# Gated units: one fp32 product from the ring in place of three fp32r products on split pieces, and seven ring slots for the experts

## What is computed

```python
def swiglu(x, w1, w3, w2):
    return (jax.nn.silu(x @ w1) * (x @ w3)) @ w2
...
    for e in range(N_EXPERTS):
        out = out + combine[:, e:e + 1].astype(t.dtype) * swiglu(t, w1[e], w3[e], w2[e])
...
        u = depthwise_conv_2(h @ w_up[l], up_conv_w[l], up_conv_b[l], 1, 1)
        gate, val = jnp.split(u, 2, axis=-1)
        x = x + (jax.nn.gelu(gate) * val) @ w_down[l]
```

## Time and profile before

| | |
|---|---|
| median of 3 runs | 2473.58 us (2473.04 to 2474.61) |
| profiled execution | 2470.8 us, span 2468.7 us |
| TensorE / VectorE / ScalarE / GpSimd busy | 89% / 58% / 46% / 51% |
| weight DMA | 485.11 MB, mean 197 GB/s |
| mean granted TensorE clock | 0.946 |

### The profile page before, as it was taken

One profiled execution on the slowest core, in us unless ns is written; L12 is line 12 of the kernel. 1 busy time (PEld: TensorE's weight loads), 2 busy tenths in 40 slices (PEclk: granted clock), 3 DMA queues, 4 the chain that ended last, 5 costly groups with the idle time before them and its releaser, 6 DMA issues.

```text
span 2468.7 us, 26815 instructions
## 1 busy us (share of the span) xinstructions
PE 2201.0 (89%) x10576; PEld 1742.6 (71%) x10576; DVE 1433.9 (58%) x1744; ACT 1140.9 (46%) x1156; POOL 1248.4 (51%) x555
## 2 busy tenths in 40 slices
PE   8988699899886898989989898999989896887998
PEld 7477488775764676767767677888767674656997
DVE  1773533337735676767857676334468576454665
ACT  2152244321421574756657474443357474344554
POOL 0333255303230695959769595455478594203553
PEclk9999899989997999999999999999999998978999
DMA  7210254532002696978969697455469696203551
GB/s 290 98 35 1 77 214 169 188 112 86 30 1 86 231 365 230 367 273 325 356 241 366 231 366 262 171 195 180 171 243 362 236 360 223 102 35 154 205 178 45
DMA packets 208105, 485.11 MB, mean 197 GB/s; under 512 B 9168, under 2 KB 13008, under 8 KB 206928
## 3 DMA queue, kind: packets, MB, share of 16 engines
q1 hardware_dynamic: 207952, 483.02, 54.3%
HBM read 481.96 MB, written 1.05 MB: 196 GB/s over the span
## 4 chain that ended last, share of the span: by engine, by line
PE 78%; DVE 13%; issue 4%; ACT 3%; SPq 1%; DMA 1%; POOL 0%; DVEq 0%; ACTq 0%
PE bank L920 19%; PE bank L922 18%; PE bank L921 18%; PE bank L549 10%; PE bank L741 4%; DVE b_arena L1215 3%; PE bank L556 3%; ACT e_hi L2012 2%; DVE e_lo L1667 2%; DVE b_arena L1209 2%; PE bank L1023 1%; PE bank L702 1%; DVE b_X L1209 1%; PE bank L1102 1%; DVE b_arena L1212 1%
## 5 line engine op out<-in xcount | busy, mean ns | idle before, releaser
L2619 POOL TENSOR_TENSOR e_lo<-b_ring,e_hi 128x512 fp32r<-128x512 f32 (+3 forms) x407 | 1096.5, 2715 | 700.7 <-ACT e_hi L2012 700.6
L1667 DVE TENSOR_TENSOR e_lo<-b_ring,e_hi 128x1536 fp32r<-128x1536 f32 (+1 forms) x403 | 794.2, 1975 | 461.3 <-ACT e_hi L2012 460.5
L2012 ACT ACTIVATE e_hi<-b_ring 128x2048 fp32r<-128x2048 f32 (+1 forms) x407 | 776.3, 1911 | 408.4 <-PE bank L922 369.8
L920 PE MATMUL bank<-e_hi,e_xh 128*128 128x512 f32 (+1 forms) x1200 | 484.2, 403 | 5.7 <-DVE e_xl L1671 1.4
L922 PE MATMUL bank<-e_hi,e_xl 128*128 128x512 f32 (+1 forms) x1200 | 471.5, 393 | 0.0
L921 PE MATMUL bank<-e_lo,e_xh 128*128 128x512 f32 (+1 forms) x1200 | 471.4, 393 | 0.0
L920 PEld LDWEIGHTS bank<-e_hi,e_xh 128*128 128x128 f32 x1200 | 230.1, 192 | 74.0 <-issue 25.2
L920 PE MATMUL bank<-e_hi,e_th 128*128 128x512 f32 x688 | 271.7, 395 | 2.5 <-DVE e_tl L1671 2.4
L922 PE MATMUL bank<-e_hi,e_tl 128*128 128x512 f32 x688 | 268.8, 391 | 0.0
L921 PE MATMUL bank<-e_lo,e_th 128*128 128x512 f32 x688 | 268.2, 390 | 0.0
L922 PEld LDWEIGHTS bank<-e_hi,e_xl 128*128 128x128 f32 x1200 | 229.6, 191 | 50.0
(11 more groups left out here) (207 smaller groups left out, 2413.3 us busy)
## 6 DMA issues: line engine op xcount, KB each, us to landing
b_ring<-in_moe_w SPq DMA_DIRECT2D x168, 2048.0 KB, 8.2
b_ring<-in_w_in SPq DMA_DIRECT2D x15, 2048.0 KB, 8.2
b_ring<-in_ffn_w SPq DMA_DIRECT2D x15, 2048.0 KB, 7.9
b_ring<-in_w_up SPq DMA_DIRECT2D x12, 2048.0 KB, 8.0
b_ring<-in_w_down SPq DMA_DIRECT2D x6, 2048.0 KB, 8.8
b_ring<-in_w_o SPq DMA_DIRECT2D x4, 2048.0 KB, 7.9
b_gain<-in_gains SPq DMA_DIRECT2D x7, 1024.0 KB, 4.8
b_ring<-in_w_out SPq DMA_DIRECT2D x2, 2048.0 KB, 8.5
```

The lines of the kernel that those rows point to most:

```text
L920: e.matmul(out, ah, bh, start=first, stop=False)
L1667: e.tensor_tensor(lo[:, 0:at], raw[:, 0:at], r32(hi[:, 0:at]), ALU.subtract).then_inc(lo_dve.sem)
L2012: return e.activation(out, x, ACT.Copy)
L2619: e.tensor_tensor(lo[:, at:], raw[:, at:], r32(hi[:, at:]), ALU.subtract).then_inc(lo_pool.sem)
```

## The change

The gated products become single fp32 matmuls on the ring's own slots; `e_hi`, `e_lo`, `e_xl`, `e_tl` and all splitting on ScalarE, VectorE and GpSimd go; GpSimd has nothing left in the gated stages. The activations are plain fp32 copies (`e_x`, `e_th`, `XT`). A use is one piece instead of two, and a slot is free when TensorE has read it (`w_read`, `up_mm`, `down_mm`). The space freed in the arena holds three more slots while the experts' weights pass (7 instead of 4). SyncE's small loads are moved, and up to two more uses are issued ahead of the gain loads in front of layer 0's feed-forward and of `last_feed`.

```diff
@@ pe
-            def three(out, ah, al, bh, bl, first, last):
-                e.matmul(out, ah, bh, start=first, stop=False)
-                e.matmul(out, ah, bl, start=False, stop=False)
-                return e.matmul(out, al, bh, start=False, stop=last)
...
+                    e.wait_ge(*ring_in(at))
                     for s in range(tiles):
                         if kind == "d":
...
+                            e.wait_ge(th_out.sem, 2 * (unit + u) + (s + 1) * inc)
+                            w2 = slot(at, 1024, w // 128)
+                            for c in range(w // 128):
                                 for h in range(2):
...
+                                    ins = e.matmul(bank[4 + 2 * s + h][:, :], e_th[s][:, c, :], w2[:, c, half(h)],
+                                                   start=u == 0 and c == 0, stop=u == n - 1 and c == w // 128 - 1)
...
+                        b, wt = bank[s] if kind == "w1" else bank[2 + s], slot(at, w)
+                        ins = sums(b[:, 0:w], [(x[s][:, c, :], wt[:, c, :]) for c in range(8)])
+                    ins.then_inc(w_read.sem)
@@ last_feed
-                                ins = three(bank[b][:, 256 * f:256 * f + 256], h3[:, c, tok(f)], l3[:, c, tok(f)],
-                                            xh2[:, :, c, :], xl2[:, :, c, :], c == 0, c == 7)
+                        ins = sums(bank[b][:, 256 * f:256 * f + 256], cols_of(w, 2 * q + f))
@@ vector, scalar and gpsimd
-                    if p + 2 < ends:
-                        split_rest(p + 2, 4 if tail and p + 2 >= at + 42 else 6)
...
-                    if p + 2 < ends:
-                        split_round(p + 2)
...
-            for ex in range(NE):
-                for i in range(42):
-                    split_rest(MOE_P + 42 * ex + i, 4 if ex and i < 2 else 6)
@@ ring
+        ring = [r[:, :] for r in fixed] + [arena[:, 22240 - SLOT * i:22240 - SLOT * (i - 1)] for i in range(NM - NR, 0, -1)]
...
+        order[4:4] = range(NR, NM)
+        for i in range(NR, NM):
+            held[i] = [wo_mm(1)]
...
+        order[:] = [i for i in order if i < NR]
```

More of the change, by code:

```diff
@@ L185, in steps_of @@
     for u in range(n + 1):
[L186 to L205, removed]
+        out += [("T", u - 1)] * (u > 0) + [("w1", u), ("w3", u)] * (u < n) + [("d", u - 1)] * (u > 0)
     return out
@@ L439, in two_blocks, with gated_uses @@
         q2_mul, lru_ix = later(sq_out, 2, 2), later(g_wide, 2, 8)
-        up_mid, up_gelu, up_h = later(XT_out, 2, 2), later(u_out, 2, 1), later(mix_cv, 2, 1)
-        up_conv, up_mul, up_l = later(w_out, 2, 2), later(v_out, 2, 1), later(o_out, 2, 1)
-        uses = []
+        up_mm, down_mm = later(inv_P, 2, 2), later(inv_XP, 2, 1)
+        up_mid, up_gelu = later(XT_out, 2, 2), later(u_out, 2, 1)
+        up_conv, up_mul = later(w_out, 2, 2), later(v_out, 2, 1)
+        uses, order, held, loads = [], list(range(NR)), {}, [0] * NM
         def use(src, *read):
[L448 to L454, removed]
+            i = order.pop(0)
+            order.append(i)
+            loads[i] += 16
+            uses.append((src, i, held.get(i, ()), (s_ring[i], loads[i])))
+            held[i] = read
+        def gated_uses(w1, w3, w2, widths):
+            n = len(widths)
             for u in range(n + 1):
@@ L1186, in last_feed @@
-                    ins.then_inc(piece.sem)
+                                for h in range(2):
+                                    ins = e.matmul(bank[4 + 2 * t + h][:, :], h4[:, 2 * c + t, :], w[:, 2 * q + c, half(h)],
+                                                   start=k == 0 and c == 0, stop=k == npair - 1 and c == 1)
+                        ins.then_inc(down_mm.sem)
+                        continue
+                    b, w = up.take(), slot(n)
+                    for f in range(2):
+                        ins = sums(bank[b][:, 256 * f:256 * f + 256], cols_of(w, 2 * q + f))
@@ L2260, in mixer, with gated @@
                 weave(mixer_attention(l), mixer_delta(l), mixer_conv(l))
-            def split_round(p):
-                raw, hi, _, _ = split_views(p, 0)
-                e.wait_ge(*pieces[p][0])
-                if p >= NH:
-                    e.wait_ge(*piece(p - NH))
-                copy(hi, raw).then_inc(w_hi.sem)
-            def gated(widths, at, unit, tiles, ends, tail=None):
-                n, p, inc = len(widths), at, 2 // tiles
-                for kind, u, hf in steps_of(widths):
+            def gated(widths, at, unit, tiles, tail=None):
+                n, inc = len(widths), 2 // tiles
+                for kind, u in steps_of(widths):
                     w = widths[u]
@@ L2705, in sp @@
             load_gain(5, rms_out(0))
[L2706 removed]
+            load(FF2_AT + 4)
             load_gain(6, rms_out(1))
```

371 lines of the change are left out of this document (124 added, 247 removed).

## The result

The changed kernel takes 2746.64 us (median of 4 runs, 2744.19 to 2751.56), the kernel before beside it 2473.31 (4 runs, 2469.98 to 2474.61): a ratio of 1.111, 95% interval 1.109 to 1.1129. That is slower by 273 us. The forecast was 2775, so the rise was put 28 us too high.

A forecast was written before the change was run, and what follows sets the result against it. TensorE was taken as the bound, with transfers nearly level in one-tile experts. Dearer products +361 us less 60 us of waits gave +301 on the 2473.6 us median: 2775 us, range 2738 to 2822.

The forecast's parts named there:

- Price of a product: Gated stages: one fp32 matmul takes 0.859 us against 0.681 for three fp32r, +0.178 per full product, +0.074 per 256-wide one.
- rival 2: Gated products: each costs four full fp32r passes, 0.908 us, giving 2885 us; chance 0.04.
- Count and sum by stage: Gated stages: 1856 full products add 330 us (layer 0 44, experts 269, last feed-forward 17), 416 narrow ones 31; together +361.
- `e_h` and `e_y`: Gated stages: TensorE's waits for these VectorE results shrink about 1 us each with VectorE idle, -19 us.
- Layer norm 0 and the last feed-forward: Their starts: without splitting, slow small operations and copies go; -6.8 and -0.7 us at the first, -6.5 and -0.8 at the last.
- Late pieces: Experts with one tile: waits for late split pieces go, 0.45 us for 6 units of 7 experts, -19 us.
- Start of the experts: First expert's selection: without ScalarE's copies and VectorE's split ahead of it, 7.2 of the 9.56 us wait goes.
- Branch stops and "seven slots ... so 0": Seams between experts: stops behind branches stay at 6 to 9 us, and the seven ring slots gain 0.
- Rival 1: Seams: the stop behind a branch falls to 2 us, gaining 48 us, for 2727 us; chance 0.10.
- Start of an expert: Transposes of `e_G` to first T, one tile: 16 x 0.178 less 1.44 us of `e_h` wait, +1.4 us.
- the term put at 0: Seams between experts: no change in time was counted there, 0 us.

The follow-up runs named there:

- the reordered kernel: Kernel before, with VectorE's products, copies and picks ahead of its splits, ScalarE's last roundings behind the norm, GpSimd's split at layer norm 0 held: 2460.92 us.
- the busy GpSimd: Changed kernel with four useless 128x1024 GpSimd subtractions beside the layer norm of layer 0: 2751.03 us, one run.
- two matmuls of three: Kernel before without the product of the tokens' high part and the weights' low part, all splitting and transfers kept: 2295.46 us.
- the load held: One weight load per seam between experts held until TensorE begins the next expert: 2461.88 us on the kernel before, 2748.86 on the changed kernel.
- the early jump: TensorE's last wait of an expert moved behind the branch: 2440.46 us on the kernel before, 2734.07 on the changed kernel.

## Why the prediction was right, and where it was off

- *Price of a product:* right. 0.860 us against 0.859, in the unit with two tiles (3.8 times the 0.227 of one fp32r matmul, so rival 2's four full ones at 0.908 did not come); the last feed-forward is 249 us as computed.
- *Count and sum by stage:* right. From the first product of layer 0's feed-forward to the next norm's transposes it is +46.3 us (245.05 against 198.77), where 44 + 2.4 were forecast. The expert with two tiles grew by 58.8, where 59.8 less a few us of waits was.
- *`e_h` and `e_y`:* -19, as forecast, and the reordered kernel shows that the cause is VectorE's queue.
- *Layer norm 0 and the last feed-forward:* 7.4 and 7.9 us (7.2 of the wait, 0.7 of the copy), near the forecast (7.5 and 7.3); the busy GpSimd and the stretched rows showed the mechanism of the first. That of the last was not tested apart.
- *Late pieces:* the step took 0.45 us of a unit where the rows leave 0.57: 17.37 - 16.8. All of it went, 0.85 us more per expert than counted with the rounding of T, some 6 in all. That splitting was its cause was not shown: moving VectorE's products ahead of its splits left the unit at 17.37, and with two matmuls of three it came to 16.56 beside a DMA at 0.97.
- *Start of the experts:* the wait fell by 7.4, where 7.2 was forecast; the stop behind the first branch fell too, from 2.94 to 0.91 us, and was not counted.
- *Branch stops and "seven slots ... so 0":* this is the step that failed, in size. The slots are worth nothing, as said. But the stops did not stay: -9.9 in TensorE's waits. The prediction took their length for that of a jump alone; part of it was time in which a weight transfer was under way, and in the changed kernel that transfer starts earlier and is nearly over at the jump. Rival 1 named a shorter stop, down to 2 us and worth 48. Its causes are not borne out (with four slots the stops are as short, and with the load held they are nearly as short over the old code); its gain came to a fifth.
- *Start of an expert:* +0.87 us where +1.4 was computed, 4 in all over seven; not followed up.

The late pieces (6), the first branch (2), the seams (9.4 by elapsed time: 7.9 of stops, 1.5 of clock) and the starts of the experts' units (4) make 21 of the 24 us by which the span's rise missed the sum. Some 3 us more in the experts stay without a cause. The mixers of layers 1 and 2, which hold no gated product, differ by -1.9 us (granted clock 0.96 against 0.95) and +2.6 (0.84 against 0.87) and nearly cancel. The forecast held because the price and the count carry most of it. That the term put at 0 came to no more than 10 us is luck: nothing in the working bounded it short of rival 1's 48. The Trainium skill (Runtime: NRT & Kernel Launch, Instruction fetch mechanics) says that a taken branch out of the window forces a DMA fetch before execution goes on. The packets of the instruction queue agree with it. That such a packet comes later beside a weight transfer is not in that rule; here it was worth up to 2 us a seam.

## What to carry to other kernels

Price a change of number format by elapsed time between two marks of a stage that already runs that form, divided by the products the program has, never by the length of single rows: that gave the rise to a tenth. Before paying for a dearer product to be rid of helper work, try to put the helper work behind what TensorE waits for: of the 88 us that the change gave back (361 - 273), order alone gave 14 at the old price, and 28 once the jump was early (2440.5 to 2412.2). Where a program jumps, let the engine jump before its last wait, and start no long transfer just ahead of the jump: moving one wait gave 32 us here, and with the order of VectorE 61.

## What was not expected of the hardware

- The stop behind the jump over the two-tile code: from VectorE's last addition to the first transposes 4.4 us with the DMA idle, 6.4 with a 2 MB transfer that still had 4 us to run, 7.2 with 4.8 us to run (the reordered kernel, where the addition is over at 1085.34). The code jumped over was the same in all three.
- The stop costs nothing if the instruction packet comes 4.4 us earlier, counted from the first y product, as it does with the early jump (1.9 us behind it instead of 6.3): the transposes follow 4.6 us behind that product, where it is 4.5 without a branch. In the changed kernel, with a weight under way by then, the early jump left a stop.
- Behind a stop the granted clock is 0.50 (1.2 GHz) for some 4 to 5.5 us, after which it is 1.00 (2.4 GHz) again; with the stop gone it does not fall. Windows of the changed kernel and of the kernel before with the early jump:

```profile
1172.30:1176.00 3.70, 3.67 (x6) 1.83 (x7) 0.42 (x1) 0.00 (x0) 0.00 (x0) 0.50 0.02 4
```

```profile
1096.50:1101.50 5.00, 4.99 (x23) 4.19 (x24) 2.09 (x2) 1.73 (x1) 0.00 (x0) 1.00 0.79 314
```

  In those 5 us the second passes 23 matmuls where the kernel before passed 13 behind its stop.
- Beside GpSimd's subtractions of 128x1024 tiles a VectorE operation on two columns takes up to 1.75 us instead of 0.17, beside those of 128x2048 tiles (the kernel before) up to 3.97.
